# First two weight-block sums of the gates' marked pairs: from an accumulating DMA in place of VectorE

## The chip, the cores and the metric

One core of one Trainium2 chip. The metric is the device time in microseconds of one execution, from the runs of the whole kernel; lower is better. The traces are of one profiled execution each.

## The reference

A batch of one sequence of 256 positions with 2048 channels goes through four layers in float32. Layers 0 and 1 are attention layers of several head kinds with a memory branch; layers 2 and 3 are a hybrid of sparse attention, a convolution and stick-breaking attention, whose three branch outputs are weighed by gates:

```python
h = rms_norm_2(x, norm_w)
proj = h @ w_in                      # gates: the last 3 * 2048 columns
...
g = jax.nn.sigmoid(gates).reshape(b, s, N_BRANCH, D_MODEL)
merged = g[:, :, 0] * y_a + g[:, :, 1] * y_b + g[:, :, 2] * y_c
return x + merged @ w_out
```

Every product of the activations (256 rows) with a weight matrix is needed once; the weights, some 560 MB, come from HBM once.

## The kernel before, in words

**Products.** A product is a `Gemm` of 512 columns. Its weights come in *fills*: 256 rows by 512 columns, 512 KB, laid as two row blocks of 128 side by side (128 partitions x 1024). For each fill SyncE issues one load into one of six `raw` slots (`raw`, line 1237), ScalarE rounds it to `wh` (`hi`, line 1591), VectorE computes the rest `wl` = raw - wh (`lo`, line 2022), and TensorE does three products (high x high, high x low, low x high) for each row block and each half of the 256 rows (`mm`). There are five pairs of `wh` and `wl`, so ScalarE is at most five fills ahead of TensorE.

**Duos.** Two gemms beside each other can form a `Duo`. For a row block pair marked with `*` in its order string, the eight block products of the two gemms are done as seven, after Strassen and Winograd: units `a`, `b`, `x`, `y` (`lay_duo`, line 766; `mm_duo`, line 1357) with 6, 6, 6 and 3 instructions on TensorE instead of 24. `a` and `b` are the two loaded fills, with blocks B11, B21 and B12, B22. `x` and `y` use sums of the weight blocks, which VectorE makes: `t_outer` (line 2040, one instruction of 128x1024: B12 - B11 and B12 - B22, into slot x), `t_inner` (2061, 128x512) and `t_last` (2066, 128x512). The sums of the activations' blocks come from `s_sum`, `s_hi` and `s_lo`, once for a layer and a marked pair number. In each of layers 2 and 3 five duos are gates, each with eight row block pairs of which four are marked: 2 x 5 x 4 = 40. After each of them come two short gemms with the output weights of a branch. Other duos (outputs, the convolution's inputs) have marked pairs too.

**Places.** In the gates the slot x is one of three: two in the tile `tmp` (its parts 0 to 3 of five, otherwise scratch of attention and of `s_sum`), one in the tile `G`. In all other duos x is one of the six `raw` slots. The sums of the activations of the layers' output duos lie in `R`, which shares its place with `G`.

**Order.** `add_steps` (its loop over fills is at line 3041) lists the steps; `Plan.settle` (line 284) puts them in an order for each engine by an estimate of each step's length and of the transfers (bytes over a fixed rate) and by ranks. So a change of a step or of an estimate can reorder every engine's program. On the chip each engine runs its list in order; an instruction that waits holds up all behind it. SyncE's list is the loads of the weights almost alone, GpSimd's has 21 instructions in all.

Of the kernel before, what the change touches and what calls it, by code (L numbers as in the profile page):

```python
# [12 lines left out]
RAW = 6  # L13
# [3 lines left out]
XS = 3  # L17
# [102 lines left out]
class Lane:  # L120
# [146 lines left out]
class Plan:  # L267
# [16 lines left out]
    def settle(self, urgency):  # L284
# [21 lines left out]
        while self.done < total:  # L306
# [113 lines left out]
class Program:  # L420
# [73 lines left out]
    def signals(self):  # L494
        sig = lambda name: Signal(self.ctx.enter_context(self.nc.semaphore(name)), self.plan)
        self.s_raw = [sig(f"s_raw{i}") for i in range(RAW)]
        self.s_mem = [sig(f"s_mem_{i}") for i in range(4)]
        self.s_memt = [sig(f"s_memt_{i}") for i in range(5)]
# [348 lines left out]
    def sums_at(self, key, q):  # L847

        kind, L = key
        i = SUMS.get(f"{kind}{L}", SUMS.get(kind)).index(q)  # L850
        if kind == "h":
            hi, lo = self.pairs["Y"][L]
            at = (16, 14)[L] + 2 * i
            hi, lo = (x[:, at:at + 2, :].rearrange("p a b -> p (a b)") for x in (hi, lo))
        elif kind == "mem":
            hi, lo = (x[:, 16 + 2 * i:18 + 2 * i, :].rearrange("p a b -> p (a b)") for x in self.pairs["Y"][0])
        elif kind == "out" and L < 2:
            hi, lo = (self.R[:, 1, 1024 * i + 512 * x:1024 * i + 512 * x + 512] for x in range(2))
        elif kind == "out":
            hi, lo = self.pairs["Y"][L]  # L860
            hi, lo = (x[:, 8 + 2 * i:10 + 2 * i, :].rearrange("p a b -> p (a b)") for x in (hi, lo))
        elif key == ("ub", 2) and i == 2 or kind == "gate" and i == 3:
            hi, lo = self.R[:, 0, 4096:4608], self.R[:, 1, 4096:4608]
        elif kind == "gate" and i > 3:
            hi, lo = (self.R[:, 5 - i, 512 * x:512 * x + 512] for x in range(2))
# [356 lines left out]


def sp_program(P, e):
    def load_memt(n):
# [5 lines left out]
    def load_mem2():  # L1231
        e.wait_ge(*P.v_in.at(("y", 3, 2)))
        if P.outs[0][0].duo:
            e.wait_ge(*P.p_mm.at(P.last_sums(("out", 0))))
        e.dma_start(P.memT, P.ins["memT"]).then_inc(*P.s_mem2.up("mem", 16))

    def raw(f):
# [27 lines left out]

    return {"load_memt": load_memt, "load_mem2": load_mem2, "raw": raw, "store": store, "stored": stored}


def pool_program(P, e):
# [60 lines left out]
    return {"zero": zero, "clear_halves": clear_halves, "load_dil": load_dil, "load_constants": load_constants, "load_gfin": load_gfin, "load_second": load_second,  # L1330
            "load_cc": load_cc, "pad": pad, "merge_add": merge_add}

# [234 lines left out]
def act_program(P, e):  # L1567
# [23 lines left out]
    def hi(f):  # L1591
# [5 lines left out]
        role = P.role[f][0] if f in P.role else None  # L1597
        if role in ("b", "x", "y"):
            e.wait_ge(*P.v_tsum.at((f - "abxy".index(role), {"b": 2, "x": 1, "y": 4}[role])))
        if role not in ("x", "y"):  # L1600
# [420 lines left out]
def dve_program(P, e):  # L2021
# [18 lines left out]
    def t_outer(f):  # L2040

        a, b, x = (P.slot[f + i] for i in range(3))
        L = P.fills[f][0].L
        if x >= RAW and P.beside[L, x - RAW][0] == f + 2:
            if x == RAW + 2:
                for w in P.y_moved(13 + 4 * (L - 2)):
                    e.wait_ge(*w)
            else:
                for i in range(2 * (x - RAW), 2 * (x - RAW) + 2):
                    P.tmp.take(("beside", L, i), i)  # L2050
                    e.wait_ge(*P.tmp.free(("beside", L, i)))
        e.wait_ge(*P.raw_loaded(f))
        e.wait_ge(*P.raw_loaded(f + 1))
        if P.leaves[f + 2] is not None:
            e.wait_ge(*P.v_lo.at(P.leaves[f + 2]))
# [3 lines left out]
        e.tensor_tensor(P.raw[x], b12, P.raws[:, s, :], ALU.subtract).then_inc(*P.v_tsum.up((f, 1)))  # L2059

    def t_inner(f):
        a, b, x = (P.raw[P.slot[f + i]] for i in range(3))
        e.wait_ge(*P.v_tsum.at((f, 1)))
        e.tensor_tensor(b[:, 0, :], b[:, 1, :], x[:, 0, :], ALU.subtract).then_inc(*P.v_tsum.up((f, 2)))

    def t_last(f):
        a, b = (P.raw[P.slot[f + i]] for i in range(2))
        e.wait_ge(*P.v_tsum.at((f, 2)))
        e.wait_ge(*P.v_lo.at(f))
        e.tensor_tensor(a[:, 1, :], a[:, 1, :], b[:, 0, :], ALU.subtract).then_inc(*P.v_tsum.up((f, 4)))  # L2070

    def s_sum(of, q):
# [15 lines left out]
        e.wait_ge(*P.v_ssum.at((*key, "a")))  # L2088
        e.tensor_tensor(s[:, 0, :], a[:, 0, 128:256], a[:, 1, 128:256], ALU.add).then_inc(*P.v_ssum.up((*key, 1)))
        e.tensor_tensor(s[:, 1, :], a[:, 0, 128:256], a[:, 0, 0:128], ALU.subtract).then_inc(*P.v_ssum.up((*key, 3)))  # L2090
        e.wait_ge(*P.v_ssum.at((*key, 1)))
        e.tensor_tensor(s[:, 2, :], s[:, 0, :], a[:, 0, 0:128], ALU.subtract).then_inc(*P.v_ssum.up((*key, 2)))
        e.wait_ge(*P.v_ssum.at((*key, 2)))
# [10 lines left out]
    def duo_middle(n):  # L2104
# [3 lines left out]
        e.wait_ge(*P.p_mm.at(d.last["6"][0]))  # L2108
        e.tensor_tensor(T[:, 3, :], P.banks_of(d)["6"], T[:, 0, :], ALU.add).then_inc(*v.up((n, "v1")))
        P.bank.give(("duo", n, "6"), v, (n, "v1"))  # L2110
# [15 lines left out]
    def duo_end(g):  # L2126
# [5 lines left out]
        b = P.nat.buf(g)  # L2132
        e.tensor_tensor(b, b, P.gp[g % 2][:, :, :], ALU.add).then_inc(*P.v_duo.up((n, "c" + x)))

    def duo_residual(g):
# [7 lines left out]
        x = P.X[:, :, 512 * gm.part:512 * gm.part + 512]  # L2143
        e.tensor_tensor(x, P.nat.buf(g), x, ALU.add).then_inc(*P.v_duo.up((gm.duo.n, g)))

# [183 lines left out]
    def flip_x(of, c):  # L2329
# [9 lines left out]
        if of == ("x", 3):  # L2339
            e.wait_ge(*P.p_mm.at(P.last_sums(("gate", 2))))  # L2340
        if of == ("x", 2) and P.outs[1][0].duo:
            e.wait_ge(*P.p_mm.at(P.last_sums(("out", 1))))
        if c >= 2:
# [442 lines left out]
def add_steps(P):  # L2786
# [254 lines left out]
    for f, (gm, _) in enumerate(P.fills):  # L3041
# [152 lines left out]
```

## Time and profile before

| | us |
|---|---|
| median of 3 runs | 2986.84 (2985.16 to 2987.07) |
| the profiled execution's own time | 2987.06 |
| its span, first to last instruction | 2985.3 |
| TensorE busy | 2967.4 (99%) |
| VectorE busy | 2525.8 (85%) |
| ScalarE busy | 2242.2 (75%) |
| GpSimd busy | 8.3 |
| transfers | 570.34 MB, 191 GB/s on average |

In the profile L152 is the line of every matmul, L167 of every activation, L178 of every addition or subtraction of two tiles on VectorE, L184 of its operations on three operands, L231 of its transposes, L237 of every plain DMA. PE is TensorE, PEld its weight loads, DVE VectorE, ACT ScalarE, POOL GpSimd, SP SyncE; a q behind a name is its queue. A window's row gives from:to, its length, then for each of PE, PEld, DVE, ACT and POOL the busy time with the number of instructions, the granted TensorE clock as a share of full speed, the DMA engines' busy share and GB/s. A tile's buffer numbers are left out, so `raw` is any of the six slots, and `tmp<-raw` and `G<-raw` are the `t_outer` of the gates.

### The profile page before, as it was taken

Reading aid. Unit: us, or ns where it says so; the run is one execution under the profiler, and the core shown is the slowest. Engines: PE = TensorE matmul, PEld = TensorE weight load, DVE = VectorE, ACT = ScalarE, POOL = GpSimd, SP = SyncE. Lnnn points to the kernel's source line nnn. Section 1 sums busy time; section 2 is a strip of 40 time slices with the busy share of each in tenths; the row PEclk is TensorE's granted clock in tenths of the full one; section 3 lists DMA queues with packets and bytes.
Section 4 is the critical chain, followed back from the end, with each engine's and each line's share of the span. In section 5 each row is a group of like instructions: output and inputs, shape, how many; then the busy total and the mean of one; then the engine's idle time right before and its main releaser. Section 6 shows DMA issues by size and latency. Waiting matters only on the chain.

```text
span 2985.3 us, 38308 instructions
## 1 busy us (share of the span) xinstructions
PE 2967.4 (99%) x13679; PEld 2479.1 (83%) x13679; DVE 2525.8 (85%) x4023; ACT 2242.2 (75%) x3827; POOL 8.3 (0%) x21
## 2 busy tenths in 40 slices
PE   8999999999999999999999999999999999999998
PEld 7888888877888888888888888888888888888887
DVE  6778679787779899999988888888998998888887
ACT  8797686968877676799885557677778999665684
POOL 0000000000000000000000000000000000000000
PEclk9999999999999999999999999999999999999999
DMA  9656656665556575556565666666565666566565
GB/s 328 191 166 178 179 165 218 205 181 173 177 171 216 170 220 170 177 170 190 177 194 181 202 208 204 205 198 197 154 195 176 182 185 183 177 213 204 181 205 176
DMA packets 305838, 570.34 MB, mean 191 GB/s; under 512 B 18368, under 2 KB 45152, under 8 KB 305264
## 3 DMA queue, kind: packets, MB, share of 16 engines
q1 hardware_dynamic: 301728, 557.65, 59.8%
q10 hardware_dynamic: 3040, 6.42, 0.6%
q0 software_dynamic: 880, 3.83, 0.4%
q8 instruction: 108, 1.77, 0.2%
q14 instruction: 82, 0.67, 0.1%
HBM read 565.73 MB, written 2.10 MB: 190 GB/s over the span
## 4 chain that ended last, share of the span: by engine, by line
PE 96%; DVE 1%; ACT 1%; DMA 1%; issue 0%; DVEq 0%; SPq 0%; ACTq 0%
PE gp L152 83%; PE bk L152 13%; ACT G L167 1%; DVE wl L178 1%; ACT wh L167 0%; DMA raw<-in_w_in 0%; DMA raw<-in_ev_w_mem_kv 0%; DVE merged L231 0%; PE bk L155 0%; DVE merged L178 0%; DVE nat L184 0%; DVE nat L178 0%; DVE merged L184 0%; DVE raw L178 0%; DVE merged L191 0%
## 5 line engine op out<-in xcount | busy, mean ns | idle before, releaser
L167 ACT ACTIVATE wh<-raw 128x1024 fp32r<-128x1024 f32 (+2 forms) x1138 | 1148.6, 1024 | 580.6 <-PE gp L152 459.8
L178 DVE TENSOR_TENSOR wl<-raw,wh 128x1024 fp32r<-128x1024 f32 (+2 forms) x1138 | 1319.5, 1174 | 296.7 <-ACT wh L167 289.7
L152 PE MATMUL gp<-wh,Hh 128*128 128x512 f32 (+3 forms) x2130 | 825.6, 388 | 0.6 <-DVE wl L178 0.5
L152 PE MATMUL gp<-wl,Hh 128*128 128x512 f32 (+3 forms) x2130 | 818.2, 384 | 0.0
L152 PE MATMUL gp<-wh,Hl 128*128 128x512 f32 (+3 forms) x2130 | 818.0, 384 | 0.0
L152 PE MATMUL gp<-wh,Yh 128*128 128x512 f32 (+2 forms) x1676 | 651.3, 389 | 9.2 <-DVE wl L178 9.2
L152 PE MATMUL gp<-wh,Yl 128*128 128x512 f32 (+2 forms) x1676 | 646.6, 386 | 0.0
L152 PE MATMUL gp<-wl,Yh 128*128 128x512 f32 (+2 forms) x1676 | 646.6, 386 | 0.0
L152 PEld LDWEIGHTS gp<-wh,Hh 128*128 128x128 f32 x2130 | 400.2, 188 | 80.7 <-issue 2.2
L152 PEld LDWEIGHTS gp<-wh,Hl 128*128 128x128 f32 x2130 | 400.1, 188 | 78.7
L152 PEld LDWEIGHTS gp<-wl,Hh 128*128 128x128 f32 x2130 | 400.2, 188 | 76.7
L152 PEld LDWEIGHTS gp<-wh,Yh 128*128 128x128 f32 x1676 | 315.5, 188 | 71.8 <-DVE wl L178 10.1
L152 PEld LDWEIGHTS gp<-wh,Yl 128*128 128x128 f32 x1676 | 315.4, 188 | 62.2
L152 PEld LDWEIGHTS gp<-wl,Yh 128*128 128x128 f32 x1676 | 315.6, 188 | 61.1
L167 ACT ACTIVATE G<-nat 32x256 f32<-32x256 f32 (+2 forms) x672 | 264.9, 394 | 11.3 <-DVE nat L231 1.9
L184 DVE SCALAR_TENSOR_TENSOR merged<-merged,cc 128x256 f32<-128x256 f32 x480 | 201.4, 478 | 0.0
L167 ACT ACTIVATE G<-tmp 32x192 f32<-32x192 f32 (+1 forms) x416 | 153.6, 369 | 6.7 <-DVE tmp L231 1.0
L167 ACT ACTIVATE nat<-gp,small 128x512 f32<-128x512 f32 (+3 forms) x178 | 102.6, 621 | 52.3 <-PE gp L152 49.8
L167 ACT ACTIVATE G<-G 32x256 f32<-32x256 f32 (+1 forms) x284 | 117.2, 413 | 4.3 <-DVE G L231 0.3
L152 PE MATMUL bk<-G 128*128 128x128 f32 (+5 forms) x796 | 117.3, 308 | 0.0
L152 PEld LDWEIGHTS bk<-G 128*128 128x128 f32 (+2 forms) x796 | 100.2, 186 | 12.6 <-issue 4.4
L152 PE MATMUL bk<-wh,R 128*128 128x512 f32 x294 | 106.5, 389 | 0.0
(177 smaller groups left out, 2375.9 us busy)
## 6 DMA issues: line engine op xcount, KB each, us to landing
raw<-in_w_in SPq DMA_DIRECT2D x544, 512.0 KB, 4.2
raw<-in_ev_w_in SPq DMA_DIRECT2D x104, 512.0 KB, 4.3
raw<-in_od_w_in SPq DMA_DIRECT2D x80, 512.0 KB, 4.0
raw<-in_w_out SPq DMA_DIRECT2D x64, 512.0 KB, 5.2
raw<-in_ev_w_out SPq DMA_DIRECT2D x40, 512.0 KB, 4.4
raw<-in_od_w_out SPq DMA_DIRECT2D x36, 512.0 KB, 4.6
raw<-in_w_b_out SPq DMA_DIRECT2D x32, 512.0 KB, 4.9
raw<-in_w_a_out SPq DMA_DIRECT2D x32, 512.0 KB, 5.0
```

The source lines that it names most:

```text
L152: return self.e.matmul(out, l, r, start=start, stop=stop)
L167: return self.e.activation(out, in_, func, **kw)
L178: return self.sketch(157 + size(a) * 1.042) if self.e is None else self.e.tensor_tensor(out, a, b, op)
L184: return self.e.scalar_tensor_tensor(out=out, in0=a, scalar=s, in1=b, op0=op0, op1=op1)
```

## The change

- For all forty marked pairs of the gates `t_outer` is gone. In its place SyncE gets a step `blocks`: two plain loads of 256 KB, B11 and B22, into the two halves of slot x. GpSimd gets `blocks_add`: once both have landed, two accumulating transfers of 256 KB, each of B12 out of HBM, onto the halves. `t_inner` waits for the first half (and for its own fill's load), ScalarE's `hi` of unit x for both.
- An accumulating transfer can only add, so the signs of the block sums change for every duo: `t_outer` (where it stays), `t_inner` and `t_last` add, the activation sums and the ends of the duos (`duo_middle`, `duo_end`, `duo_residual`) subtract where they added, or the other way round. Their number and sizes stay.
- The waits for the room of slot x move from `t_outer` to a helper, `room_beside`; in `blocks` they stand in SyncE's list, with one more: all activation sums of the layer's gates must be there. `blocks` may be issued once the load five fills ahead of fill b has been.
- The activation sums of the output duos of layers 0 and 1 move from `R` to the tile `H`, and so wait for the last gemm that reads `H`; two waits that guarded `R` go.
- The planner counts an accumulating transfer as 1.63 times its bytes and all transfers at 360 in place of 400 bytes per ns.

```diff
-BY_DMA = ()
+NTH_BY_DMA = (0, 1, 2, 3, 4)
+AHEAD = 5
+BLOCKS_BY_DMA = (("gate", 2), ("gate", 3))
+BY_DMA = ((0, 1),)
...
     def dma_add(self, dst, src):
...
-            self.plan.step.late = 2500.0
+            self.plan.step.late, self.plan.step.dma = 2500.0, self.plan.step.dma * 1.63
...
-                dma_free = max(dma_free, t + 1300.0) + s.dma / 400.0
+                dma_free = max(dma_free, t + 1300.0) + s.dma / 360.0
...
+    def added_up(self, f):
+        d = self.role[f][1]
+        nth = [u for u in d.units if self.role[u][0] == "a"].index(f)
+        return d.sums in BLOCKS_BY_DMA and nth in NTH_BY_DMA and self.slot[f + 2] >= RAW
+
+    def first_sums(self, f, *halves):
+
+        if self.added_up(f):
+            return [self.s_xadd[self.slot[f + 2] - RAW][h].at(f) for h in halves]
+        return [self.v_tsum.at((f, 1))]
...
         elif kind == "out" and L < 2:
-            hi, lo = (self.R[:, 1, 1024 * i + 512 * x:1024 * i + 512 * x + 512] for x in range(2))
+            hi, lo = (x[:, 8 + 2 * i:10 + 2 * i, :].rearrange("p a b -> p (a b)") for x in self.pairs["H"][L])
...
         if key in (("out", 0), ("out", 1)):
-            return [self.v_in.at((("y", 3, 2), ("y", 8, 0))[L])]
+            return [self.p_mm.at(self.h_end[L].end)]
...
+def room_beside(P, e, f):
+
+    x, L, d = P.slot[f + 2], P.fills[f][0].L, P.role[f][1]
+    if x >= RAW and P.added_up(f):
+        e.wait_ge(*P.v_s.at(*((d.sums, q) for q in SUMS[d.sums[0]])))
...
+    def blocks(f):
+
+        (a, j), b, x = P.fills[f], P.fills[f + 1][0], P.slot[f + 2]
+        e.behind("raw", P.loaded_before[f + 1 - AHEAD])
+        room_beside(P, e, f)
+        for h, gm in enumerate((a, b)):
+            k, c = 256 * j + 128 * h, gm.ranges[0][0]
+            e.dma_start(P.raw[x][:, h, :], gm.w[k:k + 128, c:c + 512]).then_inc(*P.s_xload[x - RAW].up((f, h), 16))
...
+    def blocks_add(f):
+
+        b, j = P.fills[f + 1]
+        x, c = P.slot[f + 2], b.ranges[0][0]
+        e.wait_ge(*P.s_xload[x - RAW].at((f, 0), (f, 1)))
+        for h in range(2):
+            e.dma_add(P.raw[x][:, h, :], b.w[256 * j:256 * j + 128, c:c + 512]).then_inc(*P.s_xadd[x - RAW][h].up(f, 16))
...
     def t_inner(f):
         a, b, x = (P.raw[P.slot[f + i]] for i in range(3))
-        e.wait_ge(*P.v_tsum.at((f, 1)))
-        e.tensor_tensor(b[:, 0, :], b[:, 1, :], x[:, 0, :], ALU.subtract).then_inc(*P.v_tsum.up((f, 2)))
+        for w in P.first_sums(f, 0):
+            e.wait_ge(*w)
+        if P.added_up(f):
+            e.wait_ge(*P.raw_loaded(f + 1))
+        e.tensor_tensor(b[:, 0, :], b[:, 1, :], x[:, 0, :], ALU.add).then_inc(*P.v_tsum.up((f, 2)))
...
         if role == "a":
-            for s in ("t_outer", "t_inner", "t_last"):
+            if P.added_up(f):
+                add("sp", "blocks", f)
+                add("pool", "blocks_add", f)
+            else:
+                add("dve", "t_outer", f)
+            for s in ("t_inner", "t_last"):
                 add("dve", s, f)
```

`BY_DMA = ((0, 1),)` also switches on, in layers 2 and 3, an existing step `merge_add`: the add of one gated branch output of 512 columns (branch 0, part 1) into `merged` becomes two accumulating transfers of 256 KB from SBUF to SBUF, issued by GpSimd, where VectorE added it.

## Rows read from the trace of the kernel before

**Rows 1.** Page, parts 1 and 4: busy time; shares of the chain of waits.
```profile
PE 2967.4 (99%) x13679; PEld 2479.1 (83%) x13679; DVE 2525.8 (85%) x4023; ACT 2242.2 (75%) x3827; POOL 8.3 (0%) x21
...
PE 96%; DVE 1%; ACT 1%; DMA 1%; issue 0%; DVEq 0%; SPq 0%; ACTq 0%
```

**Rows 2.** Waits of TensorE's loads: us in total, times, longest us.
```profile
PEld gp L152 <- DVE wl L178: 11.5, 5, 8.5
PEld bk L152 <- issue: 5.0, 15, 0.6
PEld gp L152 <- issue: 2.7, 11, 0.3
```

**Rows 3.** Windows of two duos: PE, PEld, DVE, ACT, POOL, clock, DMA, GB/s.
```profile
1698.00:1739.00 41.00, 41.00 (x183) 33.95 (x182) 36.48 (x37) 25.06 (x28) 0.00 (x0) 1.00 0.59 191
1823.00:1864.00 41.00, 40.40 (x178) 32.79 (x177) 36.39 (x38) 34.54 (x51) 0.54 (x1) 1.00 0.55 181
```

**Rows 4.** The same view in the last layer.
```profile
2831.00:2872.00 41.00, 40.28 (x176) 32.45 (x175) 36.38 (x38) 34.43 (x50) 0.00 (x0) 1.00 0.58 194
```

**Rows 5.** Timeline of TensorE, 1834 to 1840: start us, us, instruction.
```profile
1837.96 0.40 PE L152 MATMUL gp<-wh,Hl 128*128 128x512 f32 x1
1838.86 0.50 PE L152 MATMUL gp<-wh,Hh 128*128 128x512 f32 x1 [0.51 <-DVE wl L178]
```

**Rows 6.** Chain of waits, 2806 to 2846: start us, us, what.
```profile
2811.76 5.92 DMA raw<-in_w_in
...
2823.12 1.17 DVE merged L231
2824.31 0.42 ACT G L167
...
2842.55 1.24 DVE wl L178
```

**Rows 7.** VectorE's groups by form, 1560 to 1890 (one layer's gates).
```profile
L178 DVE TENSOR_TENSOR tmp<-raw 128x1024 f32<-128x1024 f32 x14 | 17.1, 1223 | 6.3 <-DMA raw<-in_w_in 6.3
...
L178 DVE TENSOR_TENSOR G<-raw 128x1024 f32<-128x1024 f32 x6 | 7.3, 1222 | 1.5 <-DMA raw<-in_w_in 1.5
```

**Rows 8.** Page, part 6: loads, count, size, median us to landing.
```profile
raw<-in_w_in SPq DMA_DIRECT2D x544, 512.0 KB, 4.2
```

**Rows 9.** Transfers between 10 and 60 us, in 40 slices.
```profile
GB/s 416 418 415 403 410 415 398 415 400 413 403 411 408 408 416 415 416 397 406 415 410 406 403 413 423 403 379 352 131 328 59 338 349 228 297 354 405 405 322 83
```

**Rows 10.** Weight tile raw, 10 to 60 us: landing times.
```profile
DMA to landing us min/median/max: 3.2/6.9/11.6
```

**Rows 11.** Weight tile raw, 2570 to 2895 us: landing times.
```profile
DMA to landing us min/median/max: 3.5/4.8/6.6
```

**Rows 12.** Timeline of GpSimd.
```profile
1506.39 0.55 POOL L237 DMA_DIRECT2D cc<-in_taps  x1 [538.67 <-DVE merged L184]
1859.28 0.54 POOL L237 DMA_DIRECT2D G<-in_c_ones  x1 [352.35 <-PE bk L152]
```

**Rows 13.** Tile tab: landing times of GpSimd's transfers.
```profile
DMA to landing us min/median/max: 3.8/4.0/4.3
```

**Rows 14.** Timeline of SyncE's queue, 2745 to 2780.
```profile
2745.80 33.64 SPq L237 DMA_DIRECT2D raw<-in_w_in  x14
```

**Rows 15.** Timeline of ScalarE, 2758 to 2778.
```profile
2762.46 1.06 ACT L167 ACTIVATE wh<-raw 128x1024 fp32r<-128x1024 f32 x1 [1.68 <-PE gp L152]
...
2771.96 1.06 ACT L167 ACTIVATE wh<-raw 128x1024 fp32r<-128x1024 f32 x1 [0.30 <-PE gp L152]
```

**Rows 16.** Timeline of VectorE, 2750 to 2778.
```profile
2759.22 0.68 DVE L178 TENSOR_TENSOR raw<-raw,G 128x512 f32<-128x512 f32 x1
...
2763.23 0.68 DVE L178 TENSOR_TENSOR raw<-raw,tmp 128x512 f32<-128x512 f32 x1
```

**Rows 17.** Timeline of VectorE, 2530 to 2572.
```profile
2555.24 1.29 DVE L178 TENSOR_TENSOR R<-tmp,R 128x512 fp32r<-128x512 f32 x2
...
2569.27 0.69 DVE L178 TENSOR_TENSOR raw<-raw,G 128x512 f32<-128x512 f32 x1
```

More of the change, by code:

```diff
@@ L496, in signals @@
         self.s_raw = [sig(f"s_raw{i}") for i in range(RAW)]
+        self.s_xload = [sig(f"s_xload{i}") for i in range(XS)]
+        self.s_xadd = [[sig(f"s_xadd{i}{h}") for h in range(2)] for i in range(XS)]
         self.s_mem = [sig(f"s_mem_{i}") for i in range(4)]
@@ L864, in sums_at @@
         elif kind == "gate" and i > 3:
-            hi, lo = (self.R[:, 5 - i, 512 * x:512 * x + 512] for x in range(2))
+            hi, lo = (self.R[:, i - 4, 512 * x:512 * x + 512] for x in range(2))
         else:
@@ L1221, in gated @@
         return r[:, :, gr.dh * h:gr.dh * h + gr.dh]
+def room_beside(P, e, f):
+    x, L, d = P.slot[f + 2], P.fills[f][0].L, P.role[f][1]
+    if x >= RAW and P.added_up(f):
+        e.wait_ge(*P.v_s.at(*((d.sums, q) for q in SUMS[d.sums[0]])))
+    if x >= RAW and P.beside[L, x - RAW][0] == f + 2:
+        if x == RAW + 2:
+            for w in P.y_moved(13 + 4 * (L - 2)):
+                e.wait_ge(*w)
+        else:
+            for i in range(2 * (x - RAW), 2 * (x - RAW) + 2):
+                P.tmp.take(("beside", L, i), i)
+                e.wait_ge(*P.tmp.free(("beside", L, i)))
+    if P.leaves[f + 2] is not None:
+        e.wait_ge(*P.v_lo.at(P.leaves[f + 2]))
 def sp_program(P, e):
@@ L1232, in load_mem2 @@
         e.wait_ge(*P.v_in.at(("y", 3, 2)))
-        if P.outs[0][0].duo:
-            e.wait_ge(*P.p_mm.at(P.last_sums(("out", 0))))
         e.dma_start(P.memT, P.ins["memT"]).then_inc(*P.s_mem2.up("mem", 16))
@@ L1264, in stored @@
         e.wait_ge(*P.s_out[n].at("o"))
-    return {"load_memt": load_memt, "load_mem2": load_mem2, "raw": raw, "store": store, "stored": stored}
+    return {"load_memt": load_memt, "load_mem2": load_mem2, "raw": raw, "blocks": blocks, "store": store, "stored": stored}
 def pool_program(P, e):
@@ L1330, in pool_program @@
     return {"zero": zero, "clear_halves": clear_halves, "load_dil": load_dil, "load_constants": load_constants, "load_gfin": load_gfin, "load_second": load_second,
-            "load_cc": load_cc, "pad": pad, "merge_add": merge_add}
+            "load_cc": load_cc, "pad": pad, "merge_add": merge_add, "blocks_add": blocks_add}
 def pe_program(P, e):
@@ L1597, in hi @@
         role = P.role[f][0] if f in P.role else None
-        if role in ("b", "x", "y"):
-            e.wait_ge(*P.v_tsum.at((f - "abxy".index(role), {"b": 2, "x": 1, "y": 4}[role])))
+        if role == "x":
+            for w in P.first_sums(f - 2, 0, 1):
+                e.wait_ge(*w)
+        if role in ("b", "y"):
+            e.wait_ge(*P.v_tsum.at((f - "abxy".index(role), {"b": 2, "y": 4}[role])))
         if role not in ("x", "y"):
@@ L2042, in t_outer @@
         a, b, x = (P.slot[f + i] for i in range(3))
[L2043 to L2051, printed above, removed]
+        room_beside(P, e, f)
         e.wait_ge(*P.raw_loaded(f))
         e.wait_ge(*P.raw_loaded(f + 1))
-        if P.leaves[f + 2] is not None:
-            e.wait_ge(*P.v_lo.at(P.leaves[f + 2]))
         i, j = 2 * a, 2 * b + 1
@@ L2058, in t_outer @@
         b12 = P.raw[b][:, 0, :].unsqueeze(1).broadcast_to([128, 2, 512])
-        e.tensor_tensor(P.raw[x], b12, P.raws[:, s, :], ALU.subtract).then_inc(*P.v_tsum.up((f, 1)))
+        e.tensor_tensor(P.raw[x], b12, P.raws[:, s, :], ALU.add).then_inc(*P.v_tsum.up((f, 1)))
     def t_inner(f):
         a, b, x = (P.raw[P.slot[f + i]] for i in range(3))
-        e.wait_ge(*P.v_tsum.at((f, 1)))
-        e.tensor_tensor(b[:, 0, :], b[:, 1, :], x[:, 0, :], ALU.subtract).then_inc(*P.v_tsum.up((f, 2)))
+        for w in P.first_sums(f, 0):
+            e.wait_ge(*w)
+        if P.added_up(f):
+            e.wait_ge(*P.raw_loaded(f + 1))
+        e.tensor_tensor(b[:, 0, :], b[:, 1, :], x[:, 0, :], ALU.add).then_inc(*P.v_tsum.up((f, 2)))
     def t_last(f):
@@ L2069, in t_last @@
         e.wait_ge(*P.v_lo.at(f))
-        e.tensor_tensor(a[:, 1, :], a[:, 1, :], b[:, 0, :], ALU.subtract).then_inc(*P.v_tsum.up((f, 4)))
+        e.tensor_tensor(a[:, 1, :], a[:, 1, :], b[:, 0, :], ALU.add).then_inc(*P.v_tsum.up((f, 4)))
     def s_sum(of, q):
@@ L2088, in s_sum @@
         e.wait_ge(*P.v_ssum.at((*key, "a")))
[L2089 to L2090 removed]
+        e.tensor_tensor(s[:, 0, :], a[:, 1, 128:256], a[:, 0, 128:256], ALU.subtract).then_inc(*P.v_ssum.up((*key, 1)))
+        e.tensor_tensor(s[:, 1, :], a[:, 0, 0:128], a[:, 0, 128:256], ALU.subtract).then_inc(*P.v_ssum.up((*key, 3)))
         e.wait_ge(*P.v_ssum.at((*key, 1)))
[L2092 removed]
+        e.tensor_tensor(s[:, 2, :], s[:, 0, :], a[:, 0, 0:128], ALU.add).then_inc(*P.v_ssum.up((*key, 2)))
         e.wait_ge(*P.v_ssum.at((*key, 2)))
@@ L2108, in duo_middle @@
         e.wait_ge(*P.p_mm.at(d.last["6"][0]))
-        e.tensor_tensor(T[:, 3, :], P.banks_of(d)["6"], T[:, 0, :], ALU.add).then_inc(*v.up((n, "v1")))
+        e.tensor_tensor(T[:, 3, :], T[:, 0, :], P.banks_of(d)["6"], ALU.subtract).then_inc(*v.up((n, "v1")))
         P.bank.give(("duo", n, "6"), v, (n, "v1"))
@@ L2132, in duo_end @@
         b = P.nat.buf(g)
-        e.tensor_tensor(b, b, P.gp[g % 2][:, :, :], ALU.add).then_inc(*P.v_duo.up((n, "c" + x)))
+        e.tensor_tensor(b, P.gp[g % 2][:, :, :], b, ALU.add if x == "a" else ALU.subtract).then_inc(*P.v_duo.up((n, "c" + x)))
     def duo_residual(g):
@@ L2143, in duo_residual @@
         x = P.X[:, :, 512 * gm.part:512 * gm.part + 512]
-        e.tensor_tensor(x, P.nat.buf(g), x, ALU.add).then_inc(*P.v_duo.up((gm.duo.n, g)))
+        e.tensor_tensor(x, x, P.nat.buf(g), ALU.add if gm is gm.duo.a else ALU.subtract).then_inc(*P.v_duo.up((gm.duo.n, g)))
     def in_lo(of, i):
@@ L2340, in flip_x @@
             e.wait_ge(*P.p_mm.at(P.last_sums(("gate", 2))))
-        if of == ("x", 2) and P.outs[1][0].duo:
-            e.wait_ge(*P.p_mm.at(P.last_sums(("out", 1))))
         if c >= 2:
@@ L3054, in add_steps @@
         if role == "a":
-            for s in ("t_outer", "t_inner", "t_last"):
+            if P.added_up(f):
+                add("sp", "blocks", f)
+                add("pool", "blocks_add", f)
+            else:
+                add("dve", "t_outer", f)
+            for s in ("t_inner", "t_last"):
                 add("dve", s, f)
```

## The prediction

> **What bounds the kernel now.** I read the busy times first: TensorE is busy for 2967.4 of 2985.3 us, and 96% of the chain of waits lies on it, with 1% each on VectorE, ScalarE and transfers [rows 1]. So time is won only where TensorE's products stand apart, and the number of products stays. The waits of its weight loads say how much that is: 11.5 us for `wl` from VectorE, of which one wait of 8.5 us is the kernel's start, and 5.0 and 2.7 us of issue gaps [rows 2]. Without the start that is 3.0 + 5.0 + 2.7 = 10.7 us in the whole kernel, 0.36%. A difference of 0.2%, 6 us, is about what a measurement tells from none.
>
> Then the windows of the stages that change. A duo of gates lasts 41 us. An undisturbed one has 183 products with TensorE busy throughout, one each 41.00/183 = 0.224 us, at a granted clock of 1.00 [rows 3]. I went through the windows of all ten duos: eight have 182 or 183. Two, the last duo of gates in each layer, have 178 and 176 [rows 3, 4]: 5 and 7 products short, (5 + 7) x 0.224 = 2.7 us. The timeline of TensorE shows one of the gaps: a product starts 0.90 us after the one before, and waits for `wl` [rows 5]. The chain in front of the other layer's gap begins with a load, goes over a transpose of `merged` on VectorE and many moves `G` on ScalarE, and ends in a late `wl` [rows 6]. VectorE itself is busy for 36 of the 41 us [rows 3], near its limit, yet its lateness reaches TensorE only there.
>
> **What the change takes away.** In one layer's gates there are 14 + 6 = 20 `t_outer` of 1.223 us [rows 7]; both layers have 40 x 1.223 = 48.9 us. The add that goes over to `merge_add` is one instruction of the same size a layer, some 2 x 1.22 = 2.4 us, an estimate from the same rows. Of these 51 us none is on TensorE. They count only in the 2.7 us above. Between the load and the transposes of the chain [rows 6] stands a `t_outer`, which waited for that load; without it VectorE comes to the transposes at least 1.2 us sooner, and one gap is 0.90 less a step of 0.224, some 0.7 us. So I expect both groups of gaps to shrink. Bounds: 0, if the moves on ScalarE set them, and 2.7. I take 2.0, nearer the upper end, because the piece that goes is longer than the largest single gap. What is late next is ScalarE's moves, and then TensorE.
>
> **What it adds, on SyncE.** Two loads of 256 KB for each pair, 80 in all. The SyncE queue issued 14 loads in 33.64 us [rows 14], one each 2.40 us, paced by free slots. An issue of GpSimd takes 0.55 us [rows 12]; at that length the two of a pair are 1.1 us, where a marked and an unmarked pair together give SyncE 4 x 2.40 us. Behind a `blocks` that waits stand all raw loads. It waits for slot x and for the activation sums. In the last layer the last of these sums was started at 2555.24 and the first `t_inner` of the gates at 2569.27 [rows 17], 14 us on. The planner can put the `blocks` at that place, and the loads ahead of it don't wait. If the sums come later than planned, the loads wait as long; six slots of 2.40 us less a landing of 4.8 us [rows 11, 14] leave some 9.6 us of cover, an estimate. Cost 0; without cover as much as the delay, once in a layer.
>
> **On GpSimd.** 80 accumulating transfers, and 4 for `merge_add`. The issue of one took 0.54 to 0.55 us [rows 12], 84 x 0.55 = 46 us on an engine that does nothing else. Something is queued there, though: the step that loads `cc` for the last layer waited also for the second layer's last gate sums (1506.39 to 1859.28, one step of the program) [rows 12]. In the new order it must stand behind twenty `blocks_add`, so `cc` is loaded some 350 us later, where `ones` is now, at the end of the second-last layer and so ahead of the last layer's convolution. Cost 0.
>
> By the Trainium skill (SBUF — State Buffer, "Who interferes with whom") VectorE in its two-port modes locks GpSimd out of the memory that it writes descriptors to, so such a transfer can stand still behind it. The trace's issues, at 1506 and at 1859 with VectorE at work, took 0.55 and 0.54 us [rows 12]. By the page each issue could be longer by one VectorE instruction; it would stay off TensorE's path.
>
> **The latency of a sum.** One transfer after another: the load (median 4.2 us over the kernel, 4.8 us in these stages [rows 8, 11]), two issues of 0.55 us, and the accumulation, which the trace does not show. Its nearest rows: a plain transfer from GpSimd lands in 3.8 to 4.3 us [rows 13], a load in a stretch with full engines in at most 11.6 us [rows 10]. So the chain takes from 4.8 + 1.1 + 3.8 = 9.7 to 11.6 + 1.1 + 11.6 = 24.3 us. I take 13 us, near the lower end, since the engines have room (below). The time there is for it: `blocks` may go five fills before fill b, which between two neighbouring marked pairs is four loads, 4 x 2.40 = 9.6 us before b's own load; that one lands in 4.8 us; and of two neighbouring pairs one had `t_inner` at 2759.22 and b on ScalarE at 2762.46, the other at 2763.23 and 2771.96 [rows 15, 16], 3.2 and 8.7 us later. Together 17 to 23 us. So 13 us are hidden, and 24.3 would not be. If the sum is late, `t_inner` stands on VectorE with all `lo` behind it, and then TensorE waits.
>
> **The engines' room.** A duo loads 16 fills of 512 KB, 8.39 MB; `blocks` adds 4 x 0.524 = 2.10 MB, the accumulations 2.10 MB times k, where k is what an accumulated byte costs beside a plain one. The trace has no row for k; from 1 (it reads HBM once) upwards. Near the start the engines moved 397 to 423 GB/s in 25 slices of 1.25 us, 31 us on end [rows 9]; at 410, 41 us hold 0.41 x 41 = 16.8 MB. k = 1 needs 12.6 MB (307 GB/s), k = 2 14.7 MB (358 GB/s), and k = 3 16.8 MB, full. The stages between duos load 0.524 MB each 2.40 us or 218 GB/s [rows 14], so what a duo leaves behind is caught up there. I take k = 2: hidden.
>
> By the Trainium skill (DMA: Bandwidth & Descriptors, "Specifications") a core gets about 358 GB/s out of HBM, which would make k = 2 the limit, not k = 3. The trace disagrees: 416 GB/s [rows 9]; the measurement decides.
>
> **Elsewhere.** Signs cost nothing: same instructions, same sizes. The activation sums of the outputs of layers 0 and 1 wait for the last gemm that reads `H`. The order strings have 13 unmarked half pairs of 12 products before the first mark, 13 x 12 x 0.224 = 35 us in which to make them. Cost 0. `merge_add` holds its buffer for a landing instead of 1.2 us; the next user comes a duo, 41 us, later. The reorder of all lists: between -1 and +4 us, the gaps of one such stall above; I take 0.
>
> **The sum.** 2987.06 (the profiled execution) - 2.0 = 2985.1 us. The runs shown have their median 0.2 us lower, which I leave: 2985.1.
>
> **The rivals.**
> (1) The gaps stay, or new ones of the same size come with the new order: the 2.7 us are set by ScalarE's moves in the chain [rows 6]. Time 2987 to 2990. For it: the number of moves does not change. Against: the piece taken out.
> (2) Slower: the sums are late in neighbouring pairs. Place: `t_inner` on VectorE, waiting for the accumulation. It decides from a chain of 17 us; for it is that two transfers and an idle engine stand one behind the other, and that landing reached 11.6 us [rows 10]; against it, 4.8 us in these stages [rows 11]. Price: at 19 us, 2 us late less some 1 us that the prepared fills cover, in about two pairs of each duo: 20 x 1 = 20 us, 3005; at 17.5 us a third, 2993. The same end comes with k of 4 or more, when the transfers fill up: 18.9 MB in a duo at 410 GB/s are 46 us, 5 more than 41, of which the stage after it takes up most.
> (3) Faster than forecast: VectorE's freedom lets the planner close all gaps in the waits of the loads, 10.7 us [rows 2]: 2976.4. Against: most of these are outside the gates and named issue, which VectorE doesn't set.
> (4) The change does not do what it says, because a pair has no slot x outside `raw`: all 40 have one (the rows show `tmp` and `G` in all 20 of a layer [rows 7]). No chance of its own.
>
> **How the numbers follow.** Forecast 0.47, rival 1 0.31, rival 2 0.16, rival 3 0.06. Faster by over 0.2% (below 2980.9) holds rival 3: 0.06. Within: forecast and rival 1, 0.78. Slower (above 2992.8): rival 2, 0.16. Range: the forecast's bounds are 2984.4 to 2987; with rival 1 up to 2990; to leave no more than 2 in 10 out I go down to 2982, and up into the cheap end of rival 2, 2994.
>
> **What would show it.** `tmp<-raw` and `G<-raw` gone, VectorE some 51 us less busy, 42 MB more moved, GpSimd with 84 more issues. Windows of the last gate duos with 182 or 183 products: the gain is right. The others keep 183: right that nothing is hidden badly. A row "DVE raw" or "ACT wh" waiting for a transfer `tmp<-in_w_in` for several us, and duos below 180 products: rival 2. A landing of the accumulation of over 11 us would make my 13 us wrong; a busy share of the engines near 1 in the duos, my k.

## The result and the profile after

The changed kernel takes 3030.11 us (median of 4 runs, 3025.57 to 3032.84) against 2986.95 us before: ratio 1.0143, 95% interval 1.0131 to 1.0156. It is slower by 43 us. The forecast of 2985.1 us was wrong, and so was its range, which ended at 2994.

The page of the changed kernel, busy times, queues and chain:

```profile
span 3023.7 us, 38482 instructions
PE 2977.7 (98%) x13679; PEld 2485.7 (82%) x13679; DVE 2479.8 (82%) x3981; ACT 2242.2 (74%) x3827; POOL 80.8 (3%) x105
...
q1 hardware_dynamic: 313248, 578.63, 60.4%
q0 software_dynamic: 12976, 25.85, 4.9%
...
PE 86%; issue 5%; DMA 4%; DVE 3%; ACT 1%; POOL 0%; SPq 0%; DVEq 0%; ACTq 0%
```

TensorE is as busy as before but for 10 us, in a span that is 38 us longer, and its share of the chain fell from 96% [rows 1] to 86%. What came in is `issue` and transfers, though VectorE has 46 us less to do. The waits of TensorE's products, of VectorE's sums and of GpSimd's issues say where (us in total, times, longest):

```profile
PE gp L155 <- DVE nat L187: 15.2, 4, 7.6
PE bk L155 <- DVE wl L181: 9.6, 4, 5.2
PE gp L155 <- DVE wl L181: 8.6, 1, 8.6
PE gp L155 <- DVE merged L187: 4.6, 4, 1.8
DVE raw L181 <- DMA tmp<-in_w_in: 35.4, 8, 11.3
DVE raw L181 <- DMA raw<-in_w_in: 30.6, 16, 4.5
DVE raw L181 <- DMA G<-in_w_in: 17.5, 6, 4.9
POOL tmp L247 <- issue: 205.0, 41, 7.7
POOL G L247 <- issue: 110.8, 22, 6.9
```

The third row is the start of the kernel, as in [rows 2]; the others are new (before, only `t_outer` waited for weight loads on VectorE, 7.6 and 5.7 us in all). L187 makes `nat`, and TensorE doesn't wait for it because that instruction is long: it stands on VectorE behind a sum that waits for an accumulated tile (`tmp`, `G`). The worst place, on the timelines of GpSimd, VectorE and TensorE (start, length, and in brackets the idle time before it and who ended it):

```profile
1688.21 0.86 POOL L247 DMA_DIRECT2D G<-in_w_in  x1 [6.04 <-issue]
1695.74 0.86 POOL L247 DMA_DIRECT2D tmp<-in_w_in  x1 [6.67 <-issue]
1700.90 0.86 POOL L247 DMA_DIRECT2D tmp<-in_w_in  x1 [4.30 <-issue]
1705.69 0.86 POOL L247 DMA_DIRECT2D tmp<-in_w_in  x1 [3.93 <-issue]
...
1709.84 0.69 DVE L181 TENSOR_TENSOR raw<-raw,tmp 128x512 f32<-128x512 f32 x1 [5.47 <-DMA tmp<-in_w_in]
1710.45 1.22 DVE L187 SCALAR_TENSOR_TENSOR nat<-nat,gp 128x1024 f32<-128x1024 f32 x1
...
1703.82 0.39 PE L155 MATMUL gp<-wh,Hl 128*128 128x512 f32 x1
1711.81 0.77 PE L155 MATMUL gp<-wh,Hh 128*128 128x512 f32 x1 [7.61 <-DVE nat L187]
```

Read it upwards. TensorE stood for 7.61 us for `nat`; `nat` is the instruction right behind the `t_inner` of 1709.84, which had waited 5.47 us for its sum; and that sum was issued at 1705.69, because GpSimd does nothing between two issues for 4 to 7 us. The transfer issued at 1700.90 landed at 1705.38, the next issue came at 1705.69. Of the 83 steps from one issue to the next none is shorter: each issue comes at least 0.31 us after the landing of the one before, and in 73 of them within 0.8 us. The 84 landed in 3.8 to 8.2 us, median 5.7.

The windows of the gates of both layers, and of two stretches around the longest stalls (us, then busy time and count by engine, granted clock, share of the DMA engines, GB/s):

```profile
1560.00:1900.00 340.00, 322.53 (x1396) 264.06 (x1395) 252.37 (x253) 192.59 (x228) 36.45 (x43) 0.98 0.84 250
2575.00:2915.00 340.00, 328.02 (x1422) 269.28 (x1421) 253.64 (x254) 202.89 (x247) 36.21 (x42) 0.98 0.85 252
1700.00:1720.00 20.00, 12.39 (x48) 9.83 (x47) 9.49 (x11) 4.54 (x5) 3.45 (x4) 0.83 0.70 158
1780.00:1800.00 20.00, 18.07 (x69) 14.84 (x70) 15.81 (x16) 9.21 (x10) 2.59 (x3) 0.83 0.74 194
```

The kernel before had 1497 and 1495 products in the same windows, at a share of 0.61 and 0.59. Outside the gates nothing changed: from the end of the first layer's gates to the start of the next, every product starts 21.9 us later than before, and behind the second layer's gates 38.5 us. The clock adds to the loss: before it was 1.00 in all these stretches, and in these 20 us with a stall of 5 to 8 us TensorE is granted 0.83 on average, 6.8 us of them at the lower of its two levels, 1.2 GHz (from 1708.5, in the middle of the stall, and from 1780.2), and the first product after the stall takes 0.77 us, not 0.39.

### The profile page after: what moved, and what is told of

It is laid out like the page before. It is cut to its first block, busy times and chain, and to the rows that moved or that the text cites. A ratio compares the mean times of both kernels' runs of the same rounds, so it can differ in the third digit from the quotient of the medians.

```text
span 3023.7 us, 38482 instructions
## 1 busy us (share of the span) xinstructions
PE 2977.7 (98%) x13679; PEld 2485.7 (82%) x13679; DVE 2479.8 (82%) x3981; ACT 2242.2 (74%) x3827; POOL 80.8 (3%) x105
## 4 chain that ended last, share of the span: by engine, by line
PE 86%; issue 5%; DMA 4%; DVE 3%; ACT 1%; POOL 0%; SPq 0%; DVEq 0%; ACTq 0%
PE gp L155 74%; PE bk L155 12%; DMA tmp<-in_w_in 2%; DVE wl L181 2%; ACT G L170 1%; DMA G<-in_w_in 1%; DVE nat L181 0%; ACT wh L170 0%; POOL tmp L247 0%; DMA raw<-in_w_in 0%; DVE merged L187 0%; SPq L240 0%; DVE raw L181 0%; DMA raw<-in_ev_w_mem_kv 0%; PE bk L158 0%
## 5 line engine op out<-in xcount | busy, mean ns | idle before, releaser
L187 DVE SCALAR_TENSOR_TENSOR merged<-merged,cc 128x256 f32<-128x256 f32 x480 | 201.3, 478 | 0.0
L155 PE MATMUL bk<-wh,R 128*128 128x512 f32 x264 | 97.8, 398 | 5.2 <-DVE wl L181 5.2
```

Of the source, the lines that this page charges most:

```text
L155: return self.e.matmul(out, l, r, start=start, stop=stop)
L187: return self.e.scalar_tensor_tensor(out=out, in0=a, scalar=s, in1=b, op0=op0, op1=op1)
```

## The experiments

Theory A: the loss is the accumulating transfers, because only one of them is in flight at a time. Theory B: it is their bytes, which take engine time from the plain loads. Rival C: it is one of the other edits, or the new order of the lists. Each kernel starts from the changed one, unless said otherwise; the kernel before ran beside each on the same chip at 2986.5 to 2986.9 us.

**e1, the edits without the transfers.**

```diff
-BLOCKS_BY_DMA = (("gate", 2), ("gate", 3))
-BY_DMA = ((0, 1),)
+BLOCKS_BY_DMA = ()
+BY_DMA = ()
```

> The changed kernel with all its edits but the accumulating transfers (the marked pairs of the gates keep t_outer on VectorE, merge_add stays an add on VectorE): signs, places of the sums, the planner's new rates. Theory A (GpSimd's accumulating transfers go one at a time, because the room for their descriptors holds only one, and the sums come late): 2985 to 2989 us, all of the loss is in the transfers. Theory B (the reorder of all lists is a good part of the loss): 2995 us or more.

Measured 2986.76 us, ratio 1.0000 (0.9991 to 1.0010). Signs, moved activation sums and the `H` tiles cost nothing, as forecast. All 43 us are in the accumulating transfers and what comes with them.

**e2, more room for GpSimd's descriptors.** The order of every engine's instructions is the same.

```diff
-dynamic_dma_scratch_size=512)
+dynamic_dma_scratch_size=704)
```

> The changed kernel with 704 in place of 512 bytes of each partition for GpSimd's descriptors; every engine's list is the same. Theory A: the second accumulating transfer of a pair is issued 0.9 us after the first instead of 4 to 7.7 us, a pair's sums are ready some 5 us sooner, and the time falls to 2988 to 3000 us. Theory C (the 16 engines are full: an accumulated byte costs too much): both transfers of a pair are in flight but land later, and the time stays at 3020 to 3035.

Measured 3006.29 us, ratio 1.0068 (1.0053 to 1.0083), 6 us above the range expected for theory A: one number of the build takes 24 us away, and no more. The second issue of a pair now comes 0.54 us after the first, and GpSimd's issue waits, 339 us in all, are 22.5 us:

```profile
POOL G L247 <- issue: 11.9, 4, 5.4
POOL tmp L247 <- issue: 6.5, 2, 5.4
POOL merged L247 <- issue: 4.1, 2, 2.8
...
DVE raw L181 <- DMA raw<-in_w_in: 51.2, 21, 5.5
DVE raw L181 <- DMA tmp<-in_w_in: 6.9, 4, 2.5
```

VectorE's sums hardly wait for accumulated tiles now, but for the plain load of their own block b, 51.2 us. Theory A holds for 24 us in this order of the lists; 19 us are left.

**e3, the second transfer of each block plain.** It overwrites the block and does not add to it, so this kernel leaves the 80 sums out.

```diff
+def dma_plain(self, dst, src):
+    return self.dma_add(dst, src) if self.e is None else self.e.dma_start(dst, src)
...
-            e.dma_add(P.raw[x][:, h, :], b.w[256 * j:256 * j + 128, c:c + 512])...
+            e.dma_plain(P.raw[x][:, h, :], b.w[256 * j:256 * j + 128, c:c + 512])...
```

> The changed kernel in which GpSimd's second transfer of a block is a plain one: same bytes out of HBM, same waits and lists, but it overwrites the block instead of adding (the additions of the gates' block sums are left out). Theory A: a plain transfer needs fewer descriptors, so two fit, issue 0.5 us apart, and land in about 4 us: 2985 to 2995 us. Theory D (it is GpSimd's way of issuing that puts one behind the other, whatever the transfer): the gap of 4 us and more stays, and the time is within 10 us of 3030.

Measured 2989.00 us, ratio 1.0009 (0.9999 to 1.0018), at room 512. The same bytes, issues and order cost 2 us, hardly clear of the noise, when they don't accumulate: two plain transfers go out within 1.10 us and land in 5.2 us. Its queue row beside those of before gives the price of an accumulated byte:

```profile
q1 hardware_dynamic: 313248, 578.63, 61.0%
q0 software_dynamic: 7856, 25.85, 2.6%
```

Before, q0 was 3.83 MB at 0.4%. So 22.0 MB take 2.2% in this run and 4.5% in the changed kernel. Four of the 84 transfers, those of `merge_add`, still accumulate here; without their 0.2% on both sides it is 2.0% against 4.3%, k = 2.15 where I took 2.

The first number of a q0 row, the packets, says more. Less the 880 of before, an accumulating transfer of 256 KB is 12096 / 84 = 144 packets, and a plain one (6976 - 4 x 144) / 80 = 80. Against e2, which has the same order and two transfers in flight as well, this run is 17 us faster: so the accumulation itself, its longer landing (median 6.9 us in e2, 5.2 us here) and its engine time, has a part in the 19 us that e2 leaves.

**e4, each accumulation in two halves of 64 partitions.**

```diff
-            e.dma_add(P.raw[x][:, h, :], b.w[256 * j:256 * j + 128, c:c + 512])...
+            for q in range(2):
+                k, p = 256 * j + 64 * q, slice(64 * q, 64 * q + 64)
+                e.dma_add(P.raw[x][p, h, :], b.w[k:k + 64, c:c + 512])...
```

> The changed kernel with each accumulating transfer cut in two of 64 partitions; lists otherwise the same, 512 bytes of descriptors. Theory A: half a transfer takes half the room, so a second half is in flight beside the first, and the chain gets shorter though not as short as with more room: 2995 to 3015 us. Theory C and D: no gain or a loss (four issues of 0.9 us in place of two): 3028 or more.

Measured 3015.63 us, ratio 1.0097 (1.0082 to 1.0112). At the same room of 512 the halves overlap (of 163 next issues 143 come before the last landing), and 14 us come back, though GpSimd issues nearly twice as many (the upper end of the range was 3015). A half is 80 packets, as many as a plain transfer. At 512 up to three transfers of 80 packets are in flight together, 240 (here and in e3), and never two of 144; at 704 two of 144 are, 288 (e2). That fits a limit on what the transfers in flight take of that room, and not on transfers as such. Whether the room is counted in packets isn't shown.

**e5, e6 and e8: what are the 19 us left at room 704?** Respectively a start three weight buffers earlier, every second marked pair only, and `merge_add` taken out. The expectations of e6 and e13 speak of 16 of the 40 pairs; a gate duo has four marked pairs, not five, and the trace has 40 accumulations of weights, so it is 20 pairs, half of them. "Linear in the bytes" is then 2996 us for e6, and a price for each pair's chain about 3003 us for e13.

```diff
 # all three: dynamic_dma_scratch_size=704
-AHEAD = 5
+AHEAD = 8                    # e5
-NTH_BY_DMA = (0, 1, 2, 3, 4)
+NTH_BY_DMA = (0, 2)          # e6
-BY_DMA = ((0, 1),)
+BY_DMA = ()                  # e8
```

> Room for descriptors 704 as in e2, and AHEAD 8 in place of 5: a marked pair's two block loads and accumulations may start three weight buffers earlier. Theory latency (what remains in e2, some 19 us, is sums that land late, because they start too late): 2988 to 2996 us, waits of VectorE on the accumulated tile near none. Rival transfer time (what remains is that plain weight loads land 1.2 us later in the gates, since an accumulated byte takes twice the time of the DMA engines, wherever it is put): 3002 to 3010 us as in e2, landing of the plain loads still near 6.0 us.

> Room 704, and only the first and third (of five) marked pairs of each column group take their sums from the DMA (16 of 40); the others are VectorE's as before. If the remaining cost is linear in the accumulated bytes, 40 percent of e2's 19 us is left: 2994 us. If it comes from neighbouring marked pairs whose transfers pile up (the second side's mechanism in the prediction), nearly nothing is left: 2985 to 2989 us, and VectorE's waits on loads in the gates are as before.

> Room 704, and the merge of gates 0 and 1 stays VectorE's, so that GpSimd issues 80 accumulations and not 84. In e2 TensorE lost 3.4 us at merged blocks and the accumulations behind them started late. If merge_add's transfers are a notable part of what remains: 2998 to 3002 us; if not: 3004 to 3008 us.

Measured: e5 3016.15 us (1.0101, 1.0087 to 1.0115), e6 3005.45 us (1.0062, 1.0049 to 1.0074), e8 3003.20 us (1.0058, 1.0042 to 1.0073). All three fell outside what was expected of them, e8 between its two cases. An earlier start, in the order that comes with it, is worse by 10 us, so the remainder isn't won back by starting sooner. With half of the accumulated block bytes gone (e6) nearly all of it stays, so it isn't proportional to bytes or pairs either: theory B in its simple form fell. What these kernels have in common is how their order was made.

**e7, the planner counts every transfer.** The planner that writes the lists keeps the bytes of a step in one variable, and a second transfer in the step overwrites the first. `blocks` and `blocks_add` issue two.

```diff
-self.plan.step.dma = size(dst) * dst.shape[0] * 4
+self.plan.step.dma = (self.plan.step.dma or 0) + size(dst) * dst.shape[0] * 4
...
-self.plan.step.late, self.plan.step.dma = 2500.0, self.plan.step.dma * 1.63
+self.plan.step.dma = (self.plan.step.dma or 0) + size(dst) * dst.shape[0] * 4 * 2
+self.plan.step.late = 2500.0
 # and dynamic_dma_scratch_size=704
```

> Room 704, and the planner that orders the work counts both transfers of a block step and both accumulations at twice their bytes (as written it keeps only the last one of each step). Only the order of instructions changes. If the remaining cost is an order planned on too few bytes: 2988 to 2998 us. If it is the transfers themselves: within 3 us of e2's 3006 us.

Measured 2986.84 us, ratio 1.0000 (0.9991 to 1.0010). The transfers are the same 84, their bytes the same, and the loss is gone; the time lies 1 us below the range expected. The windows of its gates:

```profile
1560.00:1900.00 340.00, 339.66 (x1499) 281.01 (x1498) 271.59 (x271) 213.39 (x267) 36.15 (x43) 1.00 0.86 260
2575.00:2915.00 340.00, 339.31 (x1495) 279.97 (x1494) 274.42 (x281) 217.02 (x274) 33.08 (x38) 1.00 0.84 253
```

As many products as before, with a DMA share of 0.86 and 0.84, as high as in the changed kernel. The accumulations even land later than in the changed kernel, in 6.9 us (median) and up to 9.4 us, as in e2. What moved is seen at one place on VectorE; e2 first, then e7:

```profile
1570.19 1.23 DVE L181 TENSOR_TENSOR wl<-raw,wh 128x1024 fp32r<-128x1024 f32 x1 [0.72 <-ACT wh L170]
1575.64 0.69 DVE L181 TENSOR_TENSOR raw<-raw,tmp 128x512 f32<-128x512 f32 x1 [4.23 <-DMA raw<-in_w_in]
1576.25 1.22 DVE L187 SCALAR_TENSOR_TENSOR merged<-nat,gp 128x1024 f32<-128x1024 f32 x1
```

```profile
1571.57 1.23 DVE L181 TENSOR_TENSOR wl<-raw,wh 128x1024 fp32r<-128x1024 f32 x1 [0.72 <-ACT wh L170]
1573.12 1.22 DVE L187 SCALAR_TENSOR_TENSOR merged<-nat,gp 128x1024 f32<-128x1024 f32 x1 [0.32 <-PE gp L155]
1574.29 1.22 DVE L181 TENSOR_TENSOR wl<-tmp,wh 128x1024 fp32r<-128x1024 f32 x1
1576.56 0.69 DVE L181 TENSOR_TENSOR wl<-raw,wh 128x512 fp32r<-128x512 f32 x1 [1.05 <-ACT wh L170]
1577.17 0.69 DVE L181 TENSOR_TENSOR raw<-raw,tmp 128x512 f32<-128x512 f32 x1
```

In e2 the sum `raw<-raw,tmp` stands ahead of `merged`, waits 4.23 us for a load, and TensorE stands 3.19 us for `merged`. In e7 `merged` and two `wl` go first, and the sum finds its data there. So the 19 us need both: transfers that accumulate, and an order that doesn't reckon with them (e3 has that order without the sums and loses 2 us, e7 has the sums in another order and loses nothing).

**e11 and e12: which part of the count.**

```diff
 # e11: room 704, nothing summed
-self.plan.step.late, self.plan.step.dma = 2500.0, ...
+self.plan.step.late, self.plan.step.dma = 6000.0, ...
 # e12: e7 with the change's own factor
-... * 4 * 2
+... * 4 * 1.63
```

> Room 704, the planner counts bytes as the changed kernel does (the last transfer of a step alone), but takes an accumulation to land 6.0 us after them in place of 2.5 us: only the expected moment of the sums moves, not that of the plain weight loads. If VectorE's places for the accumulated sums are what e7 mended: 2988 to 2994 us. If the places of the plain loads' work (ScalarE's and VectorE's weight splits, which wait for loads that land 1.2 us later) are a part: 2996 to 3004 us.

> As e7, both transfers of a step counted, with the change's factor of 1.63 for an accumulated byte in place of 2. If the lost count is the fault and not the factor: 2986 to 2990 us. If the factor matters as well: 2992 to 3000 us.

Measured: e11 2993.03 us (1.0022, 1.0012 to 1.0031), e12 2990.83 us (1.0012, 1.0003 to 1.0021). e11 is in its first case, e12 just above its own. The lost count is worth some 15 of the 19 us and the factor 1.63 some 4 (e12 against e7, 2986.84; the two intervals overlap a little, so the 4 us are just at the noise). Only expecting the sums later, with the plain loads planned as before, mends 13 us; so most of it is the place of what waits for the sums. Each of these orders is a single outcome of the planner, and a difference of a few us between two of them can't be put down to one term.

**e9 and e10: can a better order heal room 512?**

```diff
-dynamic_dma_scratch_size=704)        # e9: e7 with
+dynamic_dma_scratch_size=512)
-self.plan.step.late = 2500.0         # e10: e9 with
+self.plan.step.late = 9000.0
```

> The change's own room for descriptors (512) with e7's planner, which counts every transfer. e7 took all the loss away at room 704. Theory two parts (accumulations one at a time cost by themselves, since the second sum of a pair lands some 12 us after the issue of the first, and the order counts on less): 2995 to 3008 us, GpSimd's waits of 6 to 7 us between its issues as in the changed kernel. Rival order alone (with the transfers counted, the places of VectorE's sums are late enough for the serial chain too): 2986 to 2990 us.

> As e9, and the planner takes an accumulation to land 9.0 us after its bytes in place of 2.5 us, near what room 512 gives the second of a pair. If the serial chain is harmful only because VectorE's sums stand ahead of its end in the order: 2986 to 2992 us with GpSimd still waiting 6 to 7 us at each second issue. If the chain is too long for the weight buffers wherever the sums stand: as e9 or slower, 2995 us or more.

Measured: e9 3018.84 us (1.0110, 1.0095 to 1.0125), e10 3024.89 us (1.0129, 1.0114 to 1.0144). No. In both orders, one accumulation at a time leaves 32 us or more. e9 came out 11 us above its range, and e10 is in its second case. Counting the transfers wins 11 us at room 512 (3030.11 to 3018.84) and 19 us at 704. VectorE's waits for accumulated tiles in e9 are as large as e2's were small:

```profile
DVE raw L181 <- DMA G<-in_w_in: 27.3, 6, 7.4
DVE raw L181 <- DMA tmp<-in_w_in: 20.7, 3, 12.4
```

Few waits, and long ones. GpSimd's timeline for one run of four marked pairs, e9 first (eight issues), then e7 (eight in four rows of two):

```profile
1753.77 0.88 POOL L247 DMA_DIRECT2D tmp<-in_w_in  x1 [18.54 <-DMA tmp<-in_w_in]
1760.61 0.85 POOL L247 DMA_DIRECT2D tmp<-in_w_in  x1 [5.97 <-issue]
...
1796.64 0.85 POOL L247 DMA_DIRECT2D tmp<-in_w_in  x1 [6.76 <-issue]
```

```profile
1740.84 1.73 POOL L247 DMA_DIRECT2D tmp<-in_w_in  x2 [26.47 <-DMA tmp<-in_w_in]
1751.87 1.75 POOL L247 DMA_DIRECT2D tmp<-in_w_in  x2 [9.30 <-DMA tmp<-in_w_in]
1761.33 1.72 POOL L247 DMA_DIRECT2D G<-in_w_in  x2 [7.71 <-DMA G<-in_w_in]
1773.68 1.75 POOL L247 DMA_DIRECT2D tmp<-in_w_in  x2 [10.63 <-DMA tmp<-in_w_in]
```

In e9 the eight take from 1753.77 to 1801.0, 47 us at 5.9 us each, with no rest between them. In e7 GpSimd waits for the block loads, so it keeps up: the eight issues span 33 us and the last lands after 42. So is it the rate over a run, or the length of one pair's chain?

**e13 and e14: rate or latency.**

```diff
-NTH_BY_DMA = (0, 1, 2, 3, 4)
+NTH_BY_DMA = (0, 2)          # e13: e9 with
-AHEAD = 5
+AHEAD = 8                    # e14: e9 with
```

> Room 512 and the counting planner as in e9, and only the first and third of five marked pairs take their sums from the DMA (16 of 40): each pair's chain is as long as in e9, but a run of marked pairs needs half of the accumulations. If the rate of one accumulation at a time is what costs: 2985 to 2991 us. If each pair's long chain costs: 40 percent of e9's 32 us, 2998 to 3002 us.

> e9 with AHEAD 8 in place of 5: each pair's chain may start three weight buffers earlier. If the chain's length costs: 2988 to 3005 us, waits of VectorE on accumulated tiles near none. If the rate costs, an earlier start helps only the first pairs of a run: 3010 to 3022 us.

Measured: e13 2988.38 us, ratio 1.0004 (0.9995 to 1.0014), e14 3006.99 us (1.0069, 1.0054 to 1.0084). In e13 the accumulations still go one at a time, and a pair's two take as long as in e9: issued 1740.96 and 1747.68, landed 1747.35 and 1753.86, 12.9 us. Its waits:

```profile
POOL tmp L247 <- issue: 68.9, 14, 6.7
...
PE bk L155 <- DVE wl L181: 1.4, 2, 0.7
PE gp L155 <- DVE nat L187: 0.6, 1, 0.6
```

A pair's serial chain is hidden where the next pair doesn't queue behind it. The comparison with e6 tells the order's part once more: the same pairs in the uncounted order take 3005.45 us even at room 704. So what costs at room 512 is the queueing of pairs behind each other, the rate. e14 fell between its two expectations: a start three buffers earlier, at the same rate (each issue still comes at least 0.31 us behind a landing), wins 12 of the 32 us and leaves 20. The time that a run of pairs is given counts beside the rate.

## Why the prediction was wrong

The step that failed is "The latency of a sum". It put "two issues of 0.55 us, and the accumulation" one behind the other, 13 us in all, and so took both accumulations of a pair to be in flight together. They aren't at the kernel's `dynamic_dma_scratch_size` of 512: the second is issued when the first has landed. For one pair the chain becomes 4.8 + 2 x (5.7 + 0.3) = 16.8 us, still near the 17 to 23 us that I gave it, and e13 shows that such a chain costs nothing. What the step had no term for is the rate. The four marked pairs of a duo need eight accumulations of 5.7 + 0.3 us, 48 us, where a duo lasts 41 us [rows 3]. e2, e9 and e13 show it: 24 us between rooms as the change ordered it, 32 with the transfers counted, and 1.5 us, within the noise, when every second pair drops out.

The sign was in the trace of before, in the rows of GpSimd that I left out:

```profile
69.10 0.83 POOL L237 DMA_DIRECT2D masks<-in_c_masks  x1 [67.55 <-DMA X<-in_x]
69.93 0.56 POOL L237 DMA_DIRECT2D tab<-in_c_tab  x1
73.89 0.54 POOL L237 DMA_DIRECT2D small<-in_od_sinks  x1 [3.40 <-issue]
```

The third issue stood 3.40 us for "issue" with nothing in the program to wait for. The transfer of 69.10 landed at 73.58, 0.31 us before it: the same step as between two accumulations of the changed kernel. So it waited for room. I read only lone issues [rows 12], in which it can't show.

The second failure is in "Elsewhere": "The reorder of all lists: between -1 and +4 us". The order was planned on half of the bytes of the new steps, and on 1.63 in place of 2 for an accumulated byte. With room for two accumulations that costs 19 us (e2 against e7), some 15 of them by the lost count (e12). The overwritten variable stands in the diff's own function, and I read it as if it added up.

Point by point, the rest:
- VectorE's work: 51 us less forecast. Its instructions' durations add up to 52.0 us less; the busy time, which counts overlaps once, to 46.0.
- The gain, 2.0 us in the gaps of the last gate duos: not borne out. In e7 the two windows of [rows 3] and [rows 4] have 180 and 176 products, before 178 and 176, where 182 or 183 were to show it. TensorE's gap near 1838 is 0.34 us there, before 0.51 [rows 5]; the other layer's is 0.51 us, before 0.52. The time is that of before.
- The time that the sum has, 17 to 23 us: it was counted up to ScalarE's need of fill b. `t_inner` stands 3.2 and 8.7 us before that [rows 15, 16], and in its place on VectorE it holds all behind it: in e2 4.23 us of its waiting became 3.19 us of TensorE's. So the last 3.2 to 8.7 us are cover only where nothing urgent stands behind `t_inner`, as at the place shown of e7.
- SyncE's blocks, signs, moved sums, `cc` loaded some 350 us later (at 1866.97): cost 0 forecast, 0 shown by e1 (signs and sums) and e7 (all).
- GpSimd's issues: 0.86 us each, not 0.55; 84 x 0.86 = 72 us on an idle engine, no cost (e7). By the Trainium skill (SBUF — State Buffer, "Who interferes with whom") an issue could have been longer by a VectorE instruction; in the changed kernel, with VectorE busy for 82% of the span, the 84 took 0.84 to 0.90 us, so no run here shows it. Whether VectorE was in a two-port mode beside one of them, the trace doesn't tell.
- The engines' room: k = 2.15 and hidden once the order reckons with it, right: e7 has the full bytes at no loss. The plain loads of the gates landed in 5.9 us, not 4.8 (median, in the changed kernel's first layer).
- The 358 GB/s that the prediction set against its 416: only one core runs here, so the traces don't tell what a core gets beside a second one. In the gates of e7 it is 260 and 253 GB/s.
- The accumulation alone: landed in 3.8 to 8.2 us within my bounds of 3.8 to 11.6.

Rival 2 named the place, the waiting `t_inner` with TensorE behind it, and even "two transfers and an idle engine stand one behind the other". It was priced at 20 us and given 0.16, as a matter of latency in two pairs of a duo. Two causes work there, and their prices hang on each other: the room is worth 24 us in one order and 32 in the other, the order 19 us at one room and 11 at the other. Its own price stops where queueing begins (and a third of its 20 us is 7, 2992 us, not 2993).

No version beats the kernel before. The best, e7, equals it, because VectorE's 46 us were hidden behind TensorE, which is busy for 99% of the span in both.

## What to carry to other kernels

When work moves to a queue that was nearly idle, compute its rate over the densest run, not only the latency of one transfer, and look for an "issue" wait in that queue's few rows, and at what had just landed: it shows the depth. An in-order engine that consumes the result must have it late enough in its list, and a planner must count each transfer of a step. And a cut of 46 us on an engine that isn't the bound buys nothing, while its replacement can cost.

## What the runs showed of the hardware

- At a scratch size of 512 one accumulating transfer of 256 KB is in flight at a time, while two plain ones go out within 1.10 us (e3); at 704 two accumulating ones do (e2); halves of 64 partitions overlap at 512 (e4). So an accumulating transfer takes more of that room than a plain one. In packets: 144 accumulating against 80 plain; the most in flight together were 240 at 512 and 288 at 704.
- With a full room, the next issue comes 0.31 us after a landing at the earliest (83 steps of the changed kernel).
- An accumulated byte takes 2.15 times the engine time of a plain one (4.3% against 2.0% for the 80 block transfers, 21.0 MB).
- The issue of an accumulation of 256 KB takes 0.84 to 0.90 us of GpSimd at 512, of a plain transfer of the same size 0.54 to 0.58 us (e3).
- After a stall of 5 to 8 us TensorE's granted clock averages 0.83 in the 20 us around it (1.00 in the same windows before), and products take 0.77 and 0.63 us before they are back at 0.39.
